# Hybrid encoder on one core: the meta tokens are normalised first in the embedding, and four low halves of weight slices wait for the last row tile

## The reference

```
meta = jnp.broadcast_to(meta_tokens[None].astype(x.dtype), (B, N_META, D_MODEL))
h = layer_norm(jnp.concatenate([meta, x], axis=1), emb_ln_g, emb_ln_b)
...
    y = hybrid_mixer(h, pos, w_in[l], ...)      # proj = h @ w_in, then retention and DeltaNet
    h = layer_norm(DEEPNORM_ALPHA * h + y, ln1_g[l], ln1_b[l])
    y = peer_ffn(h, ...)                        # product keys, 16 of 16384 experts a head
    h = layer_norm(DEEPNORM_ALPHA * h + y, ln2_g[l], ln2_b[l])
return h[:, N_META:]
```

## Time and profile before

| | |
|---|---|
| median of three runs | 2659.88 us |
| profiled execution, its own time | 2659.92 us |
| its span | 2658.1 us |
| mean granted TensorE clock | 0.975 |
| busy: TensorE / VectorE / ScalarE / GpSimd | 92% / 67% / 37% / 47% |
| end of `embed`: first matmul behind it | 47.43 us |

### The profile page before, as it was taken

The page is one execution under the profiler, slowest core; times in us unless marked ns, Lnnn a source line. Parts: engine busy times, 40 slices in busy tenths (PEclk is TensorE's granted clock), DMA queues, the critical chain, the costliest instruction groups (busy, mean ns, idle before and its releaser), DMA issues. The chain is left out here.

```text
span 2658.1 us, 43845 instructions
## 1 busy us (share of the span) xinstructions
PE 2457.2 (92%) x14585; PEld 1441.6 (54%) x14585; DVE 1773.1 (67%) x3383; ACT 989.6 (37%) x1737; POOL 1245.9 (47%) x740
## 2 busy tenths in 40 slices
PE   7999998978999999988979999998999799999997
PEld 5444443446888888875434555555555444444442
DVE  6223212046777777763340888898999699999999
ACT  3221322123333333323212434336888333333332
POOL 4311322222212222212413576776666588888885
PEclk9999999988999999999989999999999899999999
DMA  5311312131000111002322487787999799999996
GB/s 199 95 35 61 95 40 81 39 107 33 24 16 24 32 32 32 8 0 79 96 89 86 140 270 246 246 269 246 370 371 342 257 333 332 333 334 331 335 334 238
DMA packets 174314, 440.34 MB, mean 166 GB/s; under 512 B 17408, under 2 KB 83584, under 8 KB 174096
## 3 DMA queue, kind: packets, MB, share of 16 engines
q1 hardware_dynamic: 132752, 288.20, 31.6%
q0 software_dynamic: 36864, 134.23, 15.4%
q10 hardware_dynamic: 4608, 16.78, 1.6%
HBM read 395.11 MB, written 44.04 MB: 165 GB/s over the span
## 5 line engine op out<-in xcount | busy, mean ns | idle before, releaser
L1901 POOL TENSOR_TENSOR hid_u_lo<-hid_u,hid_u_hi 128x1024 bf16<-128x1024 f32 x128 | 295.1, 2306 | 191.1 <-ACT hid_u_hi L1885 186.6
L150 PE MATMUL bank<-hT_hi,hid_u_hi 128*128 128x384 bf16 x1024 | 335.2, 327 | 17.2 <-POOL hid_u_lo L1901 5.7
L2590 POOL TENSOR_TENSOR ex_v_lo<-ex_v,ex_v_hi 128x1024 bf16<-128x1024 f32 x128 | 306.5, 2395 | 79.1 <-ACT ex_v_hi L2569 79.1
L150 PE MATMUL bank<-hT_hi,hid_u_lo 128*128 128x384 bf16 x1024 | 335.3, 327 | 0.0
L150 PE MATMUL bank<-hT_lo,hid_u_hi 128*128 128x384 bf16 x1024 | 335.2, 327 | 0.0
L205 POOL TENSOR_TENSOR ret_w_lo<-ret_w_raw,ret_w_hi 128x1024 bf16<-128x1024 f32 x72 | 155.6, 2192 | 356.0 <-ACT ret_w_hi L200 356.0
L2548 PE MATMUL bank<-ex_v_hi,ex_gated_hi 128*128 128x512 bf16 x768 | 290.6, 378 | 10.7 <-issue 0.3
L2548 PE MATMUL bank<-ex_v_hi,ex_gated_lo 128*128 128x512 bf16 x768 | 290.9, 379 | 0.0
L2548 PE MATMUL bank<-ex_v_lo,ex_gated_hi 128*128 128x512 bf16 x768 | 290.8, 379 | 0.0
L2611 DVE TENSOR_TENSOR ex_gated<-ex_gated,ex_grid 128x128 f32<-128x128 f32 x128 | 280.0, 2188 | 0.0
L2572 ACT ACTIVATE ex_gated_hi<-ex_gated 128x384 bf16<-128x384 f32 x128 | 66.9, 522 | 341.5 <-DVE ex_gated L2611 341.5
(11 more groups left out here) (486 smaller groups left out, 5820.0 us busy)
## 6 DMA issues: line engine op xcount, KB each, us to landing
hid_u<-in_peer_u SPq DMA_DIRECT2D x128, 512.0 KB, 5.0
ex_v<-in_peer_v SPq DMA_DIRECT2D x128, 512.0 KB, 5.5
ret_w_raw<-in_w_ret SPq DMA_DIRECT2D x60, 512.0 KB, 4.1
expert_hidden<-hid_gelu SPq DMA_DIRECT2D x128, 192.0 KB, 4.3
ex_gated<-expert_hidden SPq DMA_DIRECT2D x128, 192.0 KB, 4.4
dn_w_raw<-in_w_dn SPq DMA_DIRECT2D x36, 512.0 KB, 3.5
expert_weights<-ex_grid ACTq DMA_DIRECT2D x32, 512.0 KB, 10.0
ex_weights<-expert_weights SPq DMA_DIRECT2D x64, 256.0 KB, 4.7
```

Source lines behind the costliest of these rows:

```text
L150: last = nc.tensor.matmul(out, left[l], right[r], start=start and i == 0, stop=stop and i == len(PASSES) - 1)
L1901: self.nc.gpsimd.tensor_tensor(self.us[1][:, m % 2, :, :], self.u32[:, m % RING, :, :], self.us[0][:, m % 2, :, :], ALU.subtract).then_inc ...
L2590: nc.gpsimd.tensor_tensor(vs[1][:, n % SLOTS, :], v32[:, n % RING, :], vs[0][:, n % SLOTS, :], ALU.subtract).then_inc(s["v_lo"], 1)
```

## The change

Four things are done in `embed`:

- The transfer of the meta tokens is issued first, ahead of tile 0's.
- VectorE takes the meta tokens' moments before tile 0's, and normalises them after tile 0 and before tile 0's low halves. Their own low halves come behind the normalisation of tile 1. ScalarE and TensorE follow: the meta tokens' high halves stand behind slice 1's, ahead of tile 1's root; the meta tokens are turned behind the first products.
- TensorE's order is new: tile 0 turned, slices 0 and 1 with tile 0, the meta tokens turned, and then each tile is turned ahead of slices 2 and 3 of the tile before. Slices 2 and 3 with the meta tokens come ahead of the last tile's products.
- GpSimd waits for all five finished rows (`row_ok` at 5) before the low half of slice 4, so slices 4 to 7 are held back.

Two tuples carry the order in which tiles are measured and turned, and the counts of the waits and the banks follow them. The semaphores added to `spent_loads` stand behind those that later blocks take from it.

```
+MEASURED = (NT,) + tuple(range(NT))
+TURNED = (0, NT) + tuple(range(1, NT))
...
+                sp.dma_start(hm[:, :], a["meta"]).then_inc(x_in[NT], 16)
                 tokens(0)
...
-                sp.dma_start(hm[:, :], a["meta"]).then_inc(x_in[NT], 16)
...
                 for g in range(ready):
+                    if g == 4:
+                        pool.wait_ge(row_ok, NT + 1)
                     weights.lo(pool, g, g, g // 4)
...
+                moments(NT)
                 moments(0)
                 normalise(0)
+                normalise(NT)
                 low_halves(0)
                 moments(1)
                 normalise(1)
-                for t in range(2, NT + 1):
+                low_halves(NT)
+                for t in range(2, NT):
                     moments(t)
                     low_halves(t - 1)
                     normalise(t)
-                low_halves(NT)
+                low_halves(NT - 1)
...
+                deviation(NT)
                 deviation(0)
                 split(0)
                 high_halves(0)
                 split(1)
+                high_halves(NT)
                 deviation(1)
                 split(2, 3)
...
-                deviation(NT)
-                split(6)
-                high_halves(NT)
-                split(7)
+                split(6, 7)
...
                 turned(0)
-                for t in range(NT):
+                project(0, (0, 1))
+                turned(NT)
+                for t in range(1, NT):
+                    turned(t)
+                    project(t - 1, (2, 3))
+                    if t == NT - 1:
+                        project(NT, (2, 3))
                     project(t, (0, 1))
-                    turned(t + 1)
-                    project(t, (2, 3))
-                project(NT, (2, 3))
+                project(NT - 1, (2, 3))
```

More of the change, by code:

```diff
@@ L267, in embed @@
         x_in = [core.sem(f"embed_x_in{t}") for t in range(NT + 1)]
-        core.spent_loads += x_in
         gain_in, bias_in, id_in = core.sem("embed_gain_in"), core.sem("embed_bias_in"), core.sem("ident_in")
+        core.spent_loads += x_in + [gain_in, bias_in, id_in]
         hi_ready, chain, var_ok, std_ok, row_ok = (
@@ L318, in normalise @@
                     n, row = rows(t), tile(t)
-                    dve.wait_ge(std_ok, t + 1)
+                    dve.wait_ge(std_ok, MEASURED.index(t) + 1)
                     link(nc.vector.reciprocal(rstd[0:n, t:t + 1], rstd[0:n, t:t + 1]))
@@ L332, in low_halves @@
                         part = (slice(None), slice(4 * h, 4 * h + 4), tok_cols(t))
[L333 removed]
+                        dve.wait_ge(hi_ready, 2 * TURNED.index(t) + h + 1)
                         bk.reads(f"t{t}h{h}", nc.vector.tensor_tensor(hT[1][part], half_bank(t, h), hT[0][part],
                                                                       ALU.subtract))
+                moments(NT)
                 moments(0)
                 normalise(0)
+                normalise(NT)
                 low_halves(0)
@@ L351, in deviation @@
                     n = rows(t)
-                    act.wait_ge(var_ok, t + 1)
+                    act.wait_ge(var_ok, MEASURED.index(t) + 1)
                     nc.scalar.activation(rstd[0:n, t:t + 1], mv[0:n, t, 1:2], ACT.Sqrt).then_inc(std_ok, 1)
@@ L386, in turned @@
                     n = rows(t)
-                    pe.wait_ge(row_ok, t + 1)
+                    pe.wait_ge(row_ok, TURNED.index(t) + 1)
                     for h in range(2):
@@ L418, in _ @@
                 turned(0)
-                for t in range(NT):
+                project(0, (0, 1))
[5 more added lines that the diff above has]
+                        project(NT, (2, 3))
                     project(t, (0, 1))
-                    turned(t + 1)
-                    project(t, (2, 3))
-                project(NT, (2, 3))
+                project(NT - 1, (2, 3))
 def embed_banks(core):
-    return Banks(core, [(f"t{t}h{h}", 4 + (2 * t + h) % 4) for t in range(NT + 1) for h in range(2)])
+    return Banks(core, [(f"t{t}h{h}", 4 + (2 * TURNED.index(t) + h) % 4) for t in TURNED for h in range(2)])
 def retention_banks(core):
```

## The result

| | before | changed |
|---|---|---|
| median, 22 runs each | 2655.20 us (2652.47 to 2661.46) | 2660.98 us (2657.74 to 2666.02) |
| ratio | | 1.0021, 95% interval 1.0015 to 1.0027 |
| profiled execution | 2659.92, span 2658.1 | 2661.81, span 2660.0 |
| first matmul of the next block | 47.43 | 51.75 |

The changed kernel is slower by 4 to 7 us. So the two profiled spans, 1.9 us apart, are a poor measure of the change; the ratio and the block's end are better ones.

The account below looks back on a forecast made before the run. VectorE sets the pace up to tile 1's products, TensorE behind. Tile 1's products +6.64 us less 2.58 regained gives +4.06, block end 51.5 us; added to 2659.88, forecast 2664.0 us, own range 2662.9 to 2665.2.

Parts of the forecast that it names:

- The new wait: ScalarE's queue: tile 1's root waits behind the meta tokens' high halves until 21.35 us; VectorE waits more than 3 us.
- The collision in VectorE's gap: Before tile 0's low halves, GpSimd's low half stretches the meta tokens' second large instruction to 3.04 us, not 1.28.
- The cold turn of tile 1: TensorE's clock falls in the longer waits, adding 0.3 us to tile 1's transposes (bounds 0 and 1.3).
- What comes back: TensorE behind tile 1: gaps ahead of tile 3 and the meta tokens vanish, meta transposes already done; -2.58 us.
- The hold: GpSimd's slices 4 to 7, held back, fit under TensorE's remaining 10.2 us; priced at nothing.
- The first batch: TensorE's first 48 products, taken to need the same 4.27 us at half clock.
- The transfer at the head: Meta tokens' issue ahead of tile 0's delays tile 0, its gain and bias, and the first slice by 0.45 us.
- rival B: More lost: meta tokens late (up to 1.74 us), clock rising late (1.0), or GpSimd's last low half (1); 2665.0 to 2666.7; chance 0.20.
- It passes through undiminished: Blocks behind embed start from the wait of all engines, so the whole +4.06 us reaches the total time.
- Rival D: Later blocks absorb the change and nothing is visible; chance 0.05 together with C.
- A: Collisions with GpSimd missed, each giving back 1.76 us: 2662.2 with one, 2660.5 with both; chance 0.15.
- C: Faster: tile 1's root taken at 17.8, so ScalarE's new wait is free; 2658.3, or 2660.1 with the collision; 0.05 with D.

Follow-up runs that it names:

- e1: Changed kernel with ScalarE taking tile 1's root and slices 2 and 3 ahead of the meta tokens' high halves; 1.0000 of before, block end 45.49 us.
- e5: Changed kernel with GpSimd also waiting ahead of slices 0 and 2, for the meta rows and tile 1's rows; 1.0026 of before, block end 49.57 us.
- e2: Changed kernel without GpSimd's wait before slice 4, so slices 4 to 7 aren't held back; 1.0025 of before, block end 51.56 us.
- e7: Kernel before with only the meta tokens' transfer moved to the head of SyncE's queue; 1.0002 of before, block end 45.76 us.
- e4: Kernel before with GpSimd holding slices 2, 4 and 6 for the rows of tiles 1, 2 and 3; 1.0000 of before, block end 45.50 us.
- e6: e1 and e5 together: changed kernel with tile 1's root first and holds also on slices 0 and 2; 0.9994 of before, block end 45.10 us.
- e3: Changed kernel with VectorE normalising the meta tokens behind tile 1's moments; 1.0015 of before, block end 48.75 us.
- e8: Kernel before with meta transfer behind the identity's, meta moments early, meta rows normalised behind tile 3's, slices 2, 4, 5 held; 0.9995 of before, block end 44.59 us.

## Why the prediction came out as it did

**The mechanism was right, and the agreement in the numbers is in part luck.** What the prediction named happened, each at its place. The new wait: root at 21.35 forecast, 21.57 measured, and e1 shows that without it the loss is gone. The collision in VectorE's gap: 3.04 forecast, 3.03 measured, and e5 shows that it is GpSimd. The cold turn of tile 1: 0.3 forecast, 1.97 - 1.66 = 0.31 measured. What comes back: 2.58 forecast; from the products behind tile 1 to the block's end it is 26.12 us before and 23.59 in the changed kernel, so 2.53. (The prediction calls the first of these 25.5 us; its sum doesn't use that figure.) The hold: hidden, and worth 0.6 to 1.0 us (e2), which the prediction had inside "TensorE never waits" and not as a price. The block's end was forecast at 51.5 and came at 51.75 and 50.56.

Two errors cancel on the way to the root. The first product was forecast at 16.17 and came at 15.73. The first batch was priced at "the same 4.27 us at half clock", but 4.27 is half clock only up to 16.80 in that profile and full clock behind it; in the changed kernel it took 4.87 and 4.17. The same misreading is in the bound of 1.3 for a late clock: its 0.09 us a product is the mean of the mixed batch (and 24 products at it, with the 0.3, make 1.1), the half clock's own distance in the rows is 0.107.

**One term looked off and wasn't.** The transfer at the head was priced at 0.45 us. In the profiled pair tile 0 landed 0.16 later (5.20 against 5.04). But over all profiles here it landed at 4.79 to 5.55 in the eight with the meta tokens issued first, mean 5.1, and at 4.34 to 5.04 in the five without, mean 4.6. So the 5.04 is the latest of its kind, and the pair understates the cost; the two ranges overlap, so 0.5 is an estimate. e7, with nothing else changed, has its first product and its block end 0.3 us behind those of the second and third profile of the kernel before. The meta tokens had landed at 2.90, 2.14 us after their issue, and their moments were over before tile 0 came, so rival B's first part is out. The estimate from the Trainium skill's "SBUF — State Buffer", section "Door 1: The DMA port swizzle", was 0.6 us for the 64 KB, against 0.45 of issue; the runs can't tell these two apart.

**What was mis-sized is what the prediction took from one profile of the kernel before**: "After the wait of 2.04 us the granted clock was 0.50", and with it the start from which it counts, a block end of 47.43. Four other executions with TensorE's order of before kept full clock there (two of before, e7, and e4, where tile 1 was turned with hardly a wait). Their waits were shorter, 1.15, 1.15 and 1.53 us in the first three, and in the two of before the block ended 2.0 us earlier. Part of the price of the new wait is thus the clock itself: it turns a fall that was seen in one of three profiles into one that was in every profile of a kernel with the late root. Against 45.4 the change costs 5.1 to 6.3 us at the block's end, not 4.06; 0.19 to 0.24% of the whole, and the runs say 0.21. The forecast ratio was 1.0015, the lower end of the measured interval.

That the measured time, 2660.98, is only 3 us below the forecast is luck as well: the forecast started 4.7 us too high, since the three runs that were shown lie at the upper end of their kernel's spread, and it added some 1.5 us too little. The clock in `embed` does not explain the high start: the two later profiles of the kernel before, with their block ends of 45.4, took 2658.63 and 2659.18.

**"It passes through undiminished"** holds for the whole retention block. Between its first VectorE work (47.29 and 51.60) and the first instruction of the block behind it there are 383.0 us in both kernels. VectorE's first instruction of the first and the second output block, before and then changed:

```profile
L800 DVE MEMSET ret_out_gate<- x1: 59/59/59, 430.3 to 430.3; 1x1 f32 x1
L800 DVE MEMSET dn_out_gate<- x1: 59/59/59, 1229.7 to 1229.7; 1x1 f32 x1
```

```profile
L810 DVE MEMSET ret_out_gate<- x1: 59/59/59, 434.6 to 434.6; 1x1 f32 x1
L810 DVE MEMSET dn_out_gate<- x1: 59/59/59, 1230.7 to 1230.7; 1x1 f32 x1
```

The lead of 4.3 us is whole at 430 and 1.0 at 1230. Between these two points nothing differs in the programs, and they took 795.4 to 800.0 us over all profiles; the changed kernel itself took 796.1 and 798.0. Whether a part of the shift is absorbed there is not shown either way: the kernel before took 799.4 to 800.0 in its three profiles, longer than the changed one in both of its own, but e6, whose block ends earliest but one, took 795.4. Over the whole program no absorption shows, as the ratio's 0.21% is 5.6 us and the block's end 5.1 to 6.3. Rival D was right at most in saying that later blocks vary; that the clock makes them vary was not followed up.

**The rivals.** A and C did not occur. B's parts did not occur either, yet its number, a little above 2665 against 2660, is nearer to the measured ratio than the forecast's. The chance of 0.20 for slower by over 0.2% was low: the estimate lies at 0.21%, and the interval spans the bound.

## What to carry to other kernels

When an engine's queue takes on an instruction that waits for a slower engine, look at what stands behind it: here two small copies of 16 tokens held the root that started the next 128 rows, for 4.5 us. A gap that looks free on one engine is free only if the neighbour that excludes it is idle too: GpSimd's low half made 3.03 us of 1.27. And a block's length read from one profile holds one draw of TensorE's clock; where a wait of 1 to 2 us lies on TensorE's path, read two or three executions before pricing a change of a few microseconds. When two forecast points agree with the trace, check the steps between them: here a first product 0.44 us early and a first batch 0.60 us long met in the same root.

## What the runs showed of the hardware that was not expected

After waits of 1.15 us (second and third profile of the kernel before), 1.53 (e7) and 1.75 (e1) TensorE went on at full clock. After 2.04 us it fell to 0.50 once the turn of tile 1 had begun, and after 3.24 (e5) and 4.98 to 4.99 us (changed, e2, e3) the whole turn ran at half clock, 1.97 us. Where the clock rises in the first batch varied from execution to execution: from the first to the last of the 48 products it took 3.85 us in e1 and 4.96 in the second profile of the kernel before. The Trainium skill's "TensorE: Matmul & The Clock Gate", section "What's actually happening", says that the gate's window runs freely and isn't reset when a kernel starts; by that rule one kernel has several block ends, and the three of the kernel before, 47.43, 45.41 and 45.43, agree.

A SCALAR_TENSOR_TENSOR on 16 partitions costs what one on 128 costs, alone (1.27 against 1.28 us) and beside GpSimd (3.03 against 3.02).

One that begins while GpSimd is already in a low half ends 1.1 us behind GpSimd's end, whatever is left of that low half: it took 1.89 us in e5, 1.94 in e4, 2.09 in e6 and 2.45 in e8. That fits the prediction's reading that the two exclude each other for a whole instruction.
